# A state-space scan with two homes for its decay rows, in room taken from the weights' low parts

## The reference

```
a_cum = cumsum(dt * a_head)                    # per head, in chunks of 128
decay = exp(where(lower, a_cum[t] - a_cum[s], -inf))
y_diag = einsum(C[t].B[s], decay, x[s] * dt[s])
y_off  = C[t] . h_in * exp(a_cum[t])
```

## Time and profile before

| | |
|---|---|
| median of 3 runs | 2839.94 us (2833.87 to 2840.79) |
| the profiled execution | 2844.39 us, its span 2842.7, mean granted clock 0.974 |
| TensorE (PE) busy | 2652.1 us, 93% |
| VectorE (DVE) busy | 1454.0 us, 51% |
| ScalarE (ACT) busy | 1251.4 us, 44% |
| GpSimd (POOL) busy | 81.7 us, 3% |
| chain that ended last | PE 80%, DVE 8%, ACT 5%, DMA 3%, issue 3% |

### The profile page before, as it was taken

One profiled execution on the slowest core, in us unless ns is written; L12 is line 12 of the kernel. 1 busy time (PEld: TensorE's weight loads), 2 busy tenths in 40 slices (PEclk: granted clock), 3 DMA queues, 4 the chain that ended last, 5 costly groups with the idle time before them and its releaser, 6 DMA issues.

```text
span 2842.7 us, 52629 instructions
## 1 busy us (share of the span) xinstructions
PE 2652.1 (93%) x20918; PEld 2432.3 (86%) x20918; DVE 1454.0 (51%) x2513; ACT 1251.4 (44%) x2051; POOL 81.7 (3%) x155
## 2 busy tenths in 40 slices
PE   7998999999998799999788898899989998999998
PEld 7985899999995499999777676699849896899998
DVE  3233575653425676663467778722583444433333
ACT  3335353432425644442337777722672345333321
POOL 0000000000000000000001211100000000000000
PEclk9999999999999999999989999899999999999999
DMA  6410122223321023223224544422203222222231
GB/s 180 122 67 0 45 89 93 91 96 105 112 96 45 8 75 104 96 96 105 82 86 171 201 162 158 164 97 90 82 4 131 90 84 95 73 97 98 96 103 69
DMA packets 74019, 273.97 MB, mean 96 GB/s; under 512 B 9610, under 2 KB 9642, under 8 KB 73504
## 3 DMA queue, kind: packets, MB, share of 16 engines
q1 hardware_dynamic: 60816, 217.42, 22.5%
q0 software_dynamic: 13072, 54.69, 6.2%
HBM read 264.93 MB, written 7.14 MB: 96 GB/s over the span
## 4 chain that ended last, share of the span: by engine, by line
PE 80%; DVE 8%; ACT 5%; DMA 3%; issue 3%; ACTq 0%; DVEq 0%; POOL 0%; POOLq 0%; SPq 0%
PE acc L329 67%; PE acc L360 2%; DMA res_tmp<-scratch_rows 2%; PE ps L842 1%; DMA w_raw<-in_stream 1%; PE ps L360 1%; ACT w_hi L304 1%; PE ps L444 1%; DVE big L1993 1%; DVE res_tmp L1366 1%; DVE big L1284 1%; PE ps L831 1%; PE ps L1561 1%; PE acc L856 1%; DVE x_split L1362 0%
## 5 line engine op out<-in xcount | busy, mean ns | idle before, releaser
L329 PE MATMUL acc<-x_split,w_hi 128*128 128x256 f32 x7968 | 1256.4, 280 | 23.0 <-DVE x_split L1362 10.9
L329 PEld LDWEIGHTS acc<-x_split,w_hi 128*128 128x128 f32 x7968 | 1075.2, 191 | 28.7 <-issue 21.5
L310 DVE TENSOR_TENSOR w_lo<-w_raw,w_hi 128x1024 fp32r<-128x1024 f32 x405 | 493.2, 1222 | 616.2 <-ACT w_hi L304 616.2
L329 PE MATMUL acc<-x_split,w_lo 128*128 128x256 f32 x3984 | 787.7, 279 | 0.0
L304 ACT ACTIVATE w_hi<-w_raw 128x1024 fp32r<-128x1024 f32 x405 | 425.1, 1054 | 588.4 <-PE acc L329 537.0
L329 PE MATMUL acc<-big_r,w_hi 128*128 128x256 f32 x3816 | 603.5, 279 | 12.2 <-DVE big_r L1362 4.5
L329 PEld LDWEIGHTS acc<-x_split,w_lo 128*128 128x128 f32 x3984 | 610.1, 190 | 0.0
L329 PEld LDWEIGHTS acc<-big_r,w_hi 128*128 128x128 f32 x3816 | 517.5, 190 | 14.7 <-issue 8.5
L329 PE MATMUL acc<-big_r,w_lo 128*128 128x256 f32 x1908 | 387.1, 279 | 0.0
L329 PEld LDWEIGHTS acc<-big_r,w_lo 128*128 128x128 f32 x1908 | 296.1, 190 | 0.0
L1662 ACT ACTIVATE res_tmp<-res_tmp 128x512 f32<-128x512 f32 (+3 forms) x256 | 120.9, 551 | 43.5 <-DVE res_tmp L1687 42.5
(11 more groups left out here) (280 smaller groups left out, 2444.8 us busy)
## 6 DMA issues: line engine op xcount, KB each, us to landing
w_raw<-in_stream SPq DMA_DIRECT2D x405, 512.0 KB, 3.3
res_tmp<-scratch_rows POOLq DMA_DIRECT2D x128, 320.0 KB, 5.7
scratch_bias<-res_tmp POOLq DMA_DIRECT2D x1, 2560.0 KB, 55.8
res_tmp<-in_x SPq DMA_DIRECT2D x2, 1024.0 KB, 7.6
res_tmp<-scratch_bias POOLq DMA_DIRECT2D x8, 256.0 KB, 4.3
scratch_x<-res_tmp POOLq DMA_DIRECT2D x1, 2048.0 KB, 7.0
res_tmp<-scratch_x POOLq DMA_DIRECT2D x1, 2048.0 KB, 8.2
out<-res_tmp SPq DMA_DIRECT2D x8, 256.0 KB, 2.2
```

Source lines behind the costliest of these rows:

```text
L310: dve.tensor_tensor(w_lo[:, u.slot], w_raw[:, u.slot], w_hi[:, u.slot].bitcast(F32), ALU.subtract).then_inc(lo_done, 1)
L329: mm = pe.matmul(a[:, h], w, AR[:, x + k, h], start=(k == 0 and w is wh and x == hi and h.start == 0), stop=(k == total - 1 and w is wl), ...
```

## The change

1. `w_lo` lies on the same bytes as `w_raw`: the subtraction writes over its input. The loads therefore wait for `units_used` instead of `lo_done`. The 16 KB a partition that this frees are eight slots: `RES` and `TMP` move up by four, the arena grows from 76 to 84 slots.
2. In the scan the decay rows have two homes, by the parity p of the tile: `rows_buf(p, b)` at `ROWS` + 10p + 5b. GpSimd fetches the rows of tile f when the heads of tile f-2 are done with that home, instead of f-1: `s_pv` starts at 16 instead of 8, and the waits on it are moved by eight.
3. VectorE's order in a tile is new: the first two caps and `out` ahead of the splits, the third cap and `times_cb` between the two splits, and so on.
4. ScalarE's copy of the turned x stands between the exponentials of the second and of the third chunk instead of ahead of all.

The counts and shapes of the instructions are the same; TensorE's and SyncE's order is unchanged.

The diff:

```diff
@@ -89,9 +89,9 @@
 
 XH, XL = 0, 8
 BIG = 16
-RES = 60
-TMP = 68
-N_SLOTS = 76
+RES = 64
+TMP = 72
+N_SLOTS = 84
 HALF = 256
 
 
@@ -186,15 +186,16 @@
     with ctx:
 
         base = (nc.sbuf_base + 63) // 64 * 64
-        ctx.enter_context(nc.sbuf_tensor("arena_room", [P, N_SLOTS * S + 16], F32))
+        ctx.enter_context(nc.sbuf_tensor("arena_room", [P, N_SLOTS * S + RING * BLK * P + 16], F32))
 
         def place(name, first, n, dtype):
             return first, n, nc.alloc_sbuf_tensor_at(name, [P, n, S], dtype, offset=base + first * S * 4)
         A = Slots(place("big", BIG, RES - BIG, F32), place("res_tmp", RES, N_SLOTS - RES, F32))
         AR = Slots(place("x_split", XH, BIG, F32R), place("big_r", BIG, RES - BIG, F32R))
-        w_raw = ctx.enter_context(nc.sbuf_tensor("w_raw", [P, RING, BLK * P], F32))
+
+        w_raw = nc.alloc_sbuf_tensor_at("w_raw", [P, RING, BLK * P], F32, offset=base + N_SLOTS * S * 4)
+        w_lo = nc.alloc_sbuf_tensor_at("w_lo", [P, RING, BLK * P], F32R, offset=base + N_SLOTS * S * 4)
         w_hi = ctx.enter_context(nc.sbuf_tensor("w_hi", [P, RING, BLK * P], F32R))
-        w_lo = ctx.enter_context(nc.sbuf_tensor("w_lo", [P, RING, BLK * P], F32R))
         par = ctx.enter_context(nc.sbuf_tensor("par", [P, N_PAR], F32))
         const = ctx.enter_context(nc.sbuf_tensor("const", [P, N_CONST], F32))
         small = ctx.enter_context(nc.sbuf_tensor("small", [P, 128], F32))
@@ -290,7 +291,7 @@
 
         def load_unit(sp, u, wait=True):
             if wait:
-                sp.wait_ge(lo_done, (u + (-RING)).count + 1)
+                sp.wait_ge(units_used, (u + (-RING)).count + 1)
             n = u.count
             src = dram["stream"][n] if isinstance(n, int) else dram["stream"][ds(n, 1)].rearrange("a p n -> p (a n)")
             sp.dma_start(w_raw[:, u.slot], src).then_inc(landed[u.slot], 16)
@@ -1371,9 +1372,9 @@
                 low(KD - 1)
 
 
-        BT, CT, CB, TAB, ROWS, BG = 48, 52, 60, 65, 66, 31
+        BT, CT, CB, TAB, ROWS, BG = 48, 52, 58, 63, 64, 31
         DT, DA, ONE_ROWS, R_DIAG = 56, 57, 58, 59
-        XT, XTOK, VH, VL = 56, 58, 16, 32
+        XT, XTOK, VH, VL = 46, 56, 16, 32
         SCR_ROWS, SCR_X = dram["scratch_rows"], dram["scratch_x"]
 
 
@@ -1384,12 +1385,14 @@
         upto = const[:, CONST["upto"]:CONST["upto"] + P]
         onward = const[:, CONST["onward"]:CONST["onward"] + P]
 
-        def rows_buf(b):
-            return A[:, ROWS + 5 * b:ROWS + 5 * b + 5].rearrange("p b n -> p (b n)")
-
-        def part(b, c):
-
-            return rows_buf(b)[:, BACK[c]:BACK[c] + S + P]
+        def rows_buf(p, b):
+
+            at = ROWS + 10 * p + 5 * b
+            return A[:, at:at + 5].rearrange("p b n -> p (b n)")
+
+        def part(p, b, c):
+
+            return rows_buf(p, b)[:, BACK[c]:BACK[c] + S + P]
 
         cb_packed = A[:, CB:CB + 5].rearrange("p b n -> p (b n)")
         tab = A[:, TAB].rearrange("p (k c h) -> p k c h", k=2, c=CH)
@@ -1524,12 +1527,13 @@
             pool.wait_ge(ev("s_rdiag"), 1)
 
             def body(i):
-                for c in range(CH):
-                    for b in range(2):
-                        pool.wait_ge(ev("s_pv"), 8 * i + (2 * c + b + 1))
-                        src = SCR_ROWS[ds(2 * i + b, 1), BACK[c]:BACK[c] + S + P].to_broadcast([P, S + P])
-                        pool.dma_start(part(b, c), src).then_inc(ev(f"s_row_in{b}{c}"), 16)
-            repeat(pool, SSD_TILES, body)
+                for p in range(2):
+                    for c in range(CH):
+                        for b in range(2):
+                            pool.wait_ge(ev("s_pv"), 16 * i + (8 * p + 2 * c + b + 1))
+                            src = SCR_ROWS[ds(4 * i + (2 * p + b), 1), BACK[c]:BACK[c] + S + P].to_broadcast([P, S + P])
+                            pool.dma_start(part(p, b, c), src).then_inc(ev(f"s_row_in{p}{c}"), 16)
+            repeat(pool, SSD_TILES // 2, body)
 
         CB_BANK = (3, 4, 5, 2)
 
@@ -1549,10 +1553,10 @@
                 for c in range(CH):
                     pe.wait_ge(ev("s_w"), 8 * f + (2 * c + 3))
                     for b in range(2):
-                        pe.matmul(o(b, c * P, S), x(b, c), rows_buf(b)[:, FORE[c]:FORE[c] + LEN[c]], start=(c == 0),
+                        pe.matmul(o(b, c * P, S), x(b, c), rows_buf(j % 2, b)[:, FORE[c]:FORE[c] + LEN[c]], start=(c == 0),
                                   stop=False, skip_group_check=True)
                     for b in range(2):
-                        pe.matmul(o(b, 0, LENB[c]), x(b, c), rows_buf(b)[:, BACK[c]:BACK[c] + LENB[c]],
+                        pe.matmul(o(b, 0, LENB[c]), x(b, c), rows_buf(j % 2, b)[:, BACK[c]:BACK[c] + LENB[c]],
                                   start=False, stop=(c == 3), skip_group_check=True).then_inc(ev("s_pv"), 1)
 
             def square_sum(g):
@@ -1647,15 +1651,16 @@
                     act.activation(x, x, ACT.Silu).then_inc(ev("s_xt"), 1)
                     if j == 3 and not first:
                         highs(g + (-1))
-                    act.wait_ge(ev("s_xtt"), f + 1)
-                    act.activation(A[:, XTOK + j % 2], ps[:, 2], ACT.Copy).then_inc(ev("s_xtok"), 1)
                     table_of_exp_and_ln(act)
                     if j == 1 and not first:
                         rstd(g + (-1))
                     for c in range(CH):
+                        if c == 2:
+                            act.wait_ge(ev("s_xtt"), f + 1)
+                            act.activation(A[:, XTOK + j % 2], ps[:, 2], ACT.Copy).then_inc(ev("s_xtok"), 1)
                         act.wait_ge(ev("s_cap"), 4 * f + (c + 1))
                         for b in range(2):
-                            w = rows_buf(b)
+                            w = rows_buf(j % 2, b)
                             for k, at, n in ((0, FORE[c], LEN[c]), (1, BACK[c], LENB[c])):
                                 head = g * 8 + (2 * j + b + 32 * k)
                                 x = w[:, at:at + n]
@@ -1672,29 +1677,30 @@
         def ssd_dve(dve):
             dve.wait_ge(ev("s_tab"), 2)
 
-            dve.memset(small[:, 41:42], 0.0).then_inc(ev("s_pv"), 2 * CH)
+            dve.memset(small[:, 41:42], 0.0).then_inc(ev("s_pv"), 4 * CH)
             dve.memset(small[:, 42:43], 0.0).then_inc(ev("s_w"), 1)
 
-            def cap(f, head, c):
-
-
-                for b in range(2):
-                    dve.wait_ge(ev(f"s_row_in{b}{c}"), 16 * (f + 1))
-                x = A[:, ROWS:ROWS + 10].rearrange("p (b m) n -> p b (m n)", b=2)
+            def cap(g, j, c):
+
+
+                p, head = j % 2, g * 8 + 2 * j
+                dve.wait_ge(ev(f"s_row_in{p}{c}"), 64 * g + 32 * (j // 2 + 1))
+                x = A[:, ROWS + 10 * p:ROWS + 10 * p + 10].rearrange("p (b m) n -> p b (m n)", b=2)
                 x = x[:, :, (S + 2 * P) * c:(S + 2 * P) * c + 2 * P].rearrange("p b (k n) -> p b k n", k=2)
                 own = tab[:, 1, c].rearrange("p (k h) -> p h k", k=2)
                 own = own[:, ds(head, 2)].rearrange("p h (k o) -> p h k o", o=1).to_broadcast([P, 2, 2, P])
                 dve.tensor_tensor(x, x, own, ALU.min).then_inc(ev("s_cap"), 1)
 
-            def times_cb(f, b, c):
-                dve.wait_ge(ev("s_e"), 8 * f + (2 * c + b + 1))
-                w, cb = part(b, c), cb_packed[:, BACK[c]:BACK[c] + S + P]
-                dve.tensor_tensor(w, w, cb, ALU.mult).then_inc(ev("s_w"), 1)
+            def times_cb(f, j, c):
+                for b in range(2):
+                    dve.wait_ge(ev("s_e"), 8 * f + (2 * c + b + 1))
+                    w, cb = part(j % 2, b, c), cb_packed[:, BACK[c]:BACK[c] + S + P]
+                    dve.tensor_tensor(w, w, cb, ALU.mult).then_inc(ev("s_w"), 1)
 
             def out(f, j):
 
                 v = A.at(VL, f)
-                dve.wait_ge(ev("s_pv"), 8 * f + 4 * CH)
+                dve.wait_ge(ev("s_pv"), 8 * f + 6 * CH)
                 dve.wait_ge(ev("s_xt"), f + 1)
                 dve.scalar_tensor_tensor(v, A[:, XT + j % 2], col("dskip", f), ps[:, j % 2], ALU.mult,
                                          ALU.add).then_inc(ev("s_v0"), 1)
@@ -1728,27 +1734,28 @@
                 for j in range(4):
                     f = 4 * g + j
                     uz, tz = Units(UB["ssd"] + 2 * j, g, 8), Tiles(TB["ssd"] + 2 * j, g, 8)
-                    x = A[:, XT + j % 2]
-                    conv5_dve(dve, tz + 1, f + 8, f + 8, x)
+                    conv5_dve(dve, tz + 1, f + 8, f + 8, A[:, XT + j % 2])
                     if j == 0:
                         table_diagonals(g)
+                    cap(g, j, 0)
+                    cap(g, j, 1)
+                    if j or not first:
+                        out(4 * g + (j - 1), (j - 1) % 4)
                     split_lo(dve, uz + RING)
-                    split_lo(dve, uz + 1 + RING)
                     if j == 2 and not first:
                         scaled(g + (-1))
-                    if j or not first:
```

(16 more changed lines are left out.)

6 lines of the change are left out of this document (3 added, 3 removed).

## The result

The changed kernel takes 2948.16 us (median of 4 runs, 2946.98 to 2949.75) against 2840.36 (4 runs, 2833.87 to 2843.01): ratio 1.0349, 95% interval 1.0309 to 1.0389. Its profiled execution took 2948.23, span 2946.6, mean granted clock 0.968.

The account below looks back on a forecast made before the run. TensorE was taken as the bound (80% of the chain of waits). Terms +46 +1 +20 +5 -22 = +50 on the profiled 2844.4 gave 2894, or 2890 for the median; range 2860 to 2914 us.

Parts of the forecast that it names:

- Part 1: Low parts over raw weights: late loads delay splits at stage changes, +46 us, and +1 inside the up projections.
- Part 2: Kernel start: unit 4's load falls into the 2560 KB bias transfer and TensorE stops, +20 us.
- the rivals: Gets faster, 7%; start by turns +9, at most 20%; up projections tip over, +35, 8%; rows ahead don't help, +14, 15%.
- The changes of stage: Where a split stands ahead of work TensorE awaits, the late load shows: together +46 us, ends +36 and +57.
- the clock: New stops of 3 us or more can each cost 2 us at the lower clock level: +5 us (0 to 8).
- the up projections: 130 units with 0.8 us slack: 3.3 us landings hidden, +1 us; a rival had them tip over, +35, 8%.
- The start: First late loads land late beside the bias transfer: +20 us, ends +9 and +25; TensorE stands 15 to 18 us.
- And not more: At the start, the loss stays at +20 us since units behind land close together at the transfer's end.
- the rule by turns: At the start, DMA engines alternate between queues, so the load lands under 10 us: +9 instead of +20, at most 20%.
- The scan: Decay rows fetched a tile ahead shorten it from 306 to 284 us: -22 us, ends -36 and -8.
- Part 3: In the scan, rows a tile ahead remove VectorE's 31.6 us wait: -40 at most, -22 us taken as VectorE limits.
- That just fits: In the scan, loads issued on use go out nearly two microseconds ahead of the row burst, before ScalarE's splits.

Follow-up runs that it names:

- the ring alone: Kernel before with low parts written over the raw weights and loads waiting for TensorE, scan and tensor addresses as before: 2920.65 us, ratio 1.0272.

## Why the prediction was wrong

**The step that failed: TensorE's own matmuls stood in the sum at nothing.** The sum "+46 +1 +20 +5 -22" has waits, stops and clock, and no term for the pace of the products. Part 1 and Part 2 price a unit at a fixed time, and that time was taken to stay. In its place the traces show 56.4 us from a slower pace: 18159 slow gaps instead of 5452. The change moves buffers, and moving the low part to where x begins set the slow pace nearly everywhere; moving it 64 bytes further gave 42 us back in the median, and moving the weights of the kernel before 64 bytes down cost 88. Neither the rivals nor the range had a case for it. The kernel before gave the hint: its windows above have 2550 matmuls in 300 us in one place and 2649 in another, at the same clock and 100% busy. The prediction even used both paces without a remark: a tile of 5.44 us in Part 2, and in Part 1 a bank that TensorE wants after 11.3 us, which for two units is 5.65 each.

**The changes of stage: right.** +46 and 5 for the clock, and +1 in the up projections, make 52; measured 58.1 in the change and 55.0 with the ring alone. The two sites that were tried in ScalarE's order confirm the mechanism; the others rest on the timelines. No up projection tipped over.

**The start: right in the main** (+20 forecast, 23.3 to 24.8 measured, within its ends of 9 and 25). The first stop was 14.76 us, where 15 to 18 was expected. "And not more" was wrong: a second stop of 5.07 us followed at 86.59. The loads issued there landed after 15.1 to 26.5 us, so the rule by turns didn't hold, and the run with the transfer held back shows that the transfer is the reason.

**The scan: direction right, size and reason in part wrong.** -22 forecast, -33.7 measured (-29.7 with the low part moved), inside the ends. I ascribed all of it to the second home. Some 17 to 20 come from the late loads, about 7 from the homes, and what the orders bring is too small to be told. The step of Part 3 that failed is "Now they must be issued when the unit is used ... That just fits": I counted the late loads of the scan as no loss, and they were the main gain.

**Where luck came in.** Without the pace the terms measure +48, by forecast +50. That is closer than the terms are: the stops were put 9.4 us too low and the gain of the scan 11.7 too low, and these two misses cancel.

## What to carry to other kernels

When a change moves buffers, compare matmul counts over busy time in windows that are fully busy, before and after: the busy share hides a pace. Before trading look-ahead for room, list where an engine's program has a wait for a load directly ahead of work that others wait for, and what large transfer runs beside the first late load. And if one stage profits, try whether the cheap half of the edit, confined to that stage, gives most of it.

## What the hardware showed unexpectedly

- The pace of back-to-back matmuls of 256 columns depends on where the weights lie. With x in place and the weights 0 bytes from its offset 48 of them took 5.76 us, at 32 bytes 5.68, at 96 about 5.65, at 64 and 576 bytes 5.44 or 5.65. That is up to 6% at a granted clock of 1.00. Distance from x and the weights' own address weren't told apart.
- At 64 and 576 bytes both paces occur in one execution, and change beside a stop or a single longer gap. The kernel before ran from 2828.9 to 2866.3 us, the changed kernel, slow throughout in its trace, within 2.8 us over four runs; the paces fit that, but only one execution of each was traced. What decides between them is open.
- A 512 KB load beside the 2560 KB write took 15.1 to 27.9 us instead of 3.3, in both kernels; with the write held back, 3.1 to 4.2.
- Two 512 KB loads issued into the burst of eight 320 KB row fetches took 8.3 us in the median and held back the rows by some 2 us a tile; issued ahead of it they took 3.3 to 3.5.
